# Windowed attention on Trainium2: one sequence over all key groups, v by token as weights, maps scaled before their transposes

## The reference

```python
B_HEADS = D_MODEL // HEAD_DIM          # 16, HEAD_DIM = 64
B_KV_HEADS = 4;  B_GROUP = 4
WINDOW = 128;  Q_BLOCK = 128;  CTX_LEN = 256
...
    def block(args):                    # one block of 128 queries, all groups
        qb, i = args
        ...
        s_band = jnp.einsum('bqhgd,bjhd->bhgqj', qb, kb).astype(f32) * ATTN_SCALE   # 384 neighbours
        s_band = jnp.where(mask, s_band, NEG_INF)
        s_ctx = jnp.einsum('bqhgd,bjhd->bhgqj', qb, kc).astype(f32) * ATTN_SCALE    # 256 context keys
        p = sink_softmax(jnp.concatenate([s_ctx, s_band], axis=-1)).astype(vb.dtype)
        return (jnp.einsum('bhgqj,bjhd->bqhgd', p[..., :n_ctx], vc)
                + jnp.einsum('bhgqj,bjhd->bqhgd', p[..., n_ctx:], vb))
    ...
    out_x = ox.swapaxes(0, 1).reshape(B, S, B_WIDTH) * jax.nn.silu(gx)
```

## Time and profile before

| | us |
|---|---|
| median of 3 runs | 3408.12 (3401.91 to 3419.62) |
| the profiled execution | 3403.24, span 3401.4 |
| PE busy | 3033.2 (89%) |
| DVE busy | 1758.4 (52%) |
| ACT busy | 967.5 (28%) |
| POOL busy | 1038.8 (31%) |

### The profile page before, as it was taken

How to read it: one execution, slowest core, us unless ns; L and a number is a source line. 1 busy time by engine, 2 the same in 40 slices (tenths; PEclk the granted TensorE clock), 3 DMA queues, 4 the chain that set the end, 5 groups by cost and what they waited for, 6 DMA issues and landing times. The chain is left out here.

```text
span 3401.4 us, 45638 instructions
## 1 busy us (share of the span) xinstructions
PE 3033.2 (89%) x16755; PEld 2580.1 (76%) x16755; DVE 1758.4 (52%) x2527; ACT 967.5 (28%) x1574; POOL 1038.8 (31%) x609
## 2 busy tenths in 40 slices
PE   3799978999999999989999988888896999788898
PEld 2678867877777777777878878878785777777786
DVE  5554234375445544455565257878625430555553
ACT  2122234231111111131111137767602001444431
POOL 1533300364454445423222212322333423000022
PEclk9899878999999999999999989999998999888899
DMA  2454232111111111123353322121110332222201
GB/s 81 154 167 137 79 87 68 37 61 45 37 49 54 45 37 49 31 69 114 118 170 138 110 85 86 55 87 48 34 38 6 124 121 74 58 57 57 69 28 66
DMA packets 207430, 257.50 MB, mean 76 GB/s; under 512 B 8969, under 2 KB 173102, under 8 KB 207294
## 3 DMA queue, kind: packets, MB, share of 16 engines
q1 hardware_dynamic: 191430, 190.99, 19.0%
q10 hardware_dynamic: 15872, 64.82, 4.8%
HBM read 188.87 MB, written 66.91 MB: 75 GB/s over the span
## 5 line engine op out<-in xcount | busy, mean ns | idle before, releaser
L858 PE MATMUL ps<-hh,w_parts 128*128 128x512 f32 (+2 forms) x2608 | 1020.1, 391 | 77.7 <-POOL hl L708 32.7
L859 PE MATMUL ps<-hl,w_parts 128*128 128x512 f32 (+2 forms) x2608 | 1003.3, 385 | 0.0
L860 PE MATMUL ps<-hh,w_parts 128*128 128x512 f32 (+2 forms) x2608 | 1000.8, 384 | 0.0
L669 POOL TENSOR_TENSOR w_parts<-w_raw,zero 128x1024 fp32r<-128x1024 f32 x140 | 297.7, 2127 | 1161.5 <-PE ps L860 860.5
L858 PEld LDWEIGHTS ps<-hh,w_parts 128*128 128x128 f32 x2608 | 498.9, 191 | 196.4 <-issue 68.7
L859 PEld LDWEIGHTS ps<-hl,w_parts 128*128 128x128 f32 x2608 | 501.1, 192 | 106.7 <-issue 6.0
L860 PEld LDWEIGHTS ps<-hh,w_parts 128*128 128x128 f32 x2608 | 499.4, 192 | 101.6
L671 POOL TENSOR_TENSOR w_parts<-w_raw,w_parts 128x1024 fp32r<-128x1024 f32 x140 | 339.6, 2425 | 11.0
L2415 DVE TENSOR_SCALAR_CACHE_REDUCE b_s<-ps 128x640 f32<-128x640 f32 (+1 forms) x128 | 101.3, 791 | 245.3 <-PE ps L1353 244.7
L1694 ACT ACTIVATE f_y<-f_z,convv 128x1024 f32<-128x1024 f32 x44 | 54.7, 1244 | 532.8 <-DVE f_z L2242 532.7
L858 PE MATMUL ps<-f_hi,d_hi 128*128 128x512 f32 x352 | 139.5, 396 | 20.1 <-DVE res L2279 14.0
(11 more groups left out here) (317 smaller groups left out, 4949.8 us busy)
## 6 DMA issues: line engine op xcount, KB each, us to landing
w_mod_sb<-in_w_mod SPq DMA_DIRECT2D x16, 1536.0 KB, 7.1
w_raw<-in_w_up SPq DMA_DIRECT2D x44, 512.0 KB, 3.8
w_raw<-in_a_w_in SPq DMA_DIRECT2D x32, 512.0 KB, 4.0
d_raw<-in_w_down SPq DMA_DIRECT2D x22, 512.0 KB, 4.1
w_raw<-in_w_in SPq DMA_DIRECT2D x20, 512.0 KB, 4.8
za_parts<-z_hi ACTq DMA_DIRECT2D x16, 640.0 KB, 3.0
za_parts<-z_lo ACTq DMA_DIRECT2D x16, 640.0 KB, 4.1
d_even<-za_parts SPq DMA_DIRECT2D x16, 640.0 KB, 6.8
```

The lines of the kernel that those rows point to most:

```text
L669: pool.tensor_tensor(wh[:, s], w_raw[:, s], zero[:].broadcast_to([P, KT * P]), ALU.add).then_inc(w_high[s], 1)
L858: pe.matmul(out_, w_hi, x_hi, start=start, stop=False)
L859: pe.matmul(out_, w_hi, x_lo, start=False, stop=False)
L860: return pe.matmul(out_, w_lo, x_hi, start=False, stop=stop)
```

## The change

1. `b_v` is projected by token (`project_by_token`): the activations are the weights of the product and the projection's weights are the moving operand, so v comes out with tokens on the partitions and ACT and DVE write it straight into `b_v`. Both slots of weights are used until the last token. v is neither stored to DRAM nor loaded nor transposed.
2. The loop over the groups becomes one sequence of 128 units. q is loaded in four pieces as the group before frees them, k into two buffers laid over the two slots of `w_parts`, the gate for all groups into `hl`.
3. The scores run 4 units ahead (`BA_LEAD`), `b_s` has 4 buffers in place of 3.
4. The sums are inverted for two units at a time (`ba_norm`), and GpSimd multiplies the map by it in place (`ba_scale`), before the transposes.
5. The mix handles the four heads of a block together, one block behind: v is the weights (64 columns), the transposed maps of two heads the moving operand (256 columns), and the two pairs of heads go to the lower and the upper 64 partitions of the output. The output comes out transposed, so the two transposes of `b_o` go.
6. The first split of `b_out` moves into GpSimd's stream at unit 104.

```diff
+BA_UNITS = 4 * QB * 4
+BA_LEAD = 4
+BA_MIX = ((0,), (1, 2), (3,), (4,))
...
+        b_pt = alloc(scope, "b_pt", [P, 2, 5, 4, P])
...
-        b_v = alloc(scope, "b_v", [P, TOK // 2 // P, 2, DH])
...
-        b_s = alloc(scope, "b_s", [P, 3, 5 * P])
-        b_pt = alloc(scope, "b_pt", [P, 2, 5, P])
...
+        b_v = alloc(scope, "b_v", [P, TOK // P, 4 * DH])
+        b_s = alloc(scope, "b_s", [P, BA_LEAD, 5 * P])
...
+        b_ks = [w_parts[:, p].rearrange("p a n -> p (a n)")[:, 0:2 * TOK].rearrange("p (a n) -> p a n", n=TOK) for p in range(2)]
...
-                sp.wait_ge(ba.scored, 32 * h + 1)
...
+            for s in range(2):
+                sp.wait_ge(stored[s], 16 * Z0["b_gate"][s] + 16)
+            for c in range(4):
+                ba_load_q(0, c)
+            for h in range(2):
+                sp.wait_ge(w_used[h], W0["b_out"][h] + 1)
+                ba_load_k(h)
+            for s in range(2):
+                sp.wait_ge(stored[s], 16 * (Z0["b_gate"][s] + 4) + 16)
+            for h in range(4):
+                ba_load_gate(h)
+            for h in range(1, 4):
+                for c in range(4):
+                    sp.wait_ge(ba.scored, 4 * QB * (h - 1) + 8 * (c + 1))
+                    ba_load_q(h, c)
+                if h < 3:
+                    ba_load_k(h + 1)
...
+            def ba_scale(u):
+                w = len(window_tiles(ba_unit(u)[1])) * P
+                pool.wait_ge(ba.normed, 2 * (u // 2) + 2)
+                pool.tensor_scalar(b_s[:, u % BA_LEAD, 0:w], b_s[:, u % BA_LEAD, 0:w], b_rec[:, 1, u % 4:u % 4 + 1], None, ALU.mult).then_inc(ba_scaled, 1)
...
+                cols = slice(CTX + i * P, CTX + (i + 1) * P)
+                pool.wait_ge(ba_kept, 2 * b + 2)
+                pool.tensor_tensor(hl[:, 2 * h:2 * h + 2, cols], b_y[:, b % 2], hh[:, 2 * h:2 * h + 2, cols].bitcast(F32), ALU.subtract).then_inc(ba.low, 1)
+
+            for u in range(BA_UNITS + 6):
+                if u < BA_UNITS:
+                    ba_scale(u)
+                if u == 4 * QB * 3 + 8:
+                    split(pool, W0["b_out"], 0, 0)
+                if u >= 9 and u % 4 == 1:
+                    ba_keep_low((u - 9) // 4)
+            split(pool, W0["b_out"], 0, 1)
...
+        def project_by_token(pe, name):
+
+            parts = w_parts[:, :, 1:3]
+            for s in range(2):
+                pe.wait_ge(acc_free[s], A0[name][s] + 1)
+                pe.wait_ge(w_split[s], W0[name][s] + 1 + 1)
+            for t in range(TOK // P):
+                if t >= 5:
+                    pe.wait_ge(acc_free[(t - 5) % 2], A0[name][(t - 5) % 2] + (t - 5) // 2 + 1 + 1)
+                tok = slice(t * P, (t + 1) * P)
+                got = bank(t % 5).rearrange("p (s w n) -> p s w n", s=2, w=2)
+                for k in range(KT):
+                    wk = slice(k * P, (k + 1) * P)
+                    if k == KT - 1:
+                        pe.matmul(got[:, :, 0], hl[:, k, tok], parts[:, :, 0, wk], start=False, stop=False)
+                    if k == KT - 1 and t == TOK // P - 1:
+                        for s in range(2):
+                            pe.matmul(got[:, s], hh[:, k, tok], parts[:, s, :, wk], start=False, stop=(s == 1)).then_inc(w_used[s], 1)
+                    else:
+                        last = pe.matmul(got, hh[:, k, tok], parts[:, :, :, wk], start=(k == 0), stop=(k == KT - 1))
+                    if k < KT - 1:
+                        pe.matmul(got[:, :, 0], hl[:, k, tok], parts[:, :, 0, wk], start=False, stop=False)
+                if t < TOK // P - 1:
+                    last.then_inc(v_turned, 1)
 
...
-            project(pe, "b_v", 2, ALL_SEGS)
+            project_by_token(pe, "b_v")
...
-                    for n, kt in enumerate(tiles):
-                        last = pe.matmul(bank(6 + i % 2)[:, a * DH:(a + 1) * DH], b_pt[:, u % 2, n, :], b_v[:, kt % 5, kt // 5, :],
-                                         start=(n == 0), stop=(n == len(tiles) - 1))
...
+            def ba_turn(u):
+                tiles = len(window_tiles(ba_unit(u)[1]))
+                pe.wait_ge(ba_scaled, u + 1)
+                for b, batch in enumerate((range(3), range(3, tiles))):
+                    if u:
+                        pe.wait_ge(ba_copied[b], u)
+                    for n in batch:
...
+                for c in range(2):
+                    last = pe.matmul(bank(6 + b % 2)[c * DH:(c + 1) * DH, 0:2 * P].rearrange("p (t q) -> p t q", t=2),
+                                     b_v[:, tiles[n], h * DH:(h + 1) * DH], b_pt[:, b % 2, n, c::2], start=(n == 0), stop=(n == len(tiles) - 1))
...
-                def ba_turn_output(i):
-                    pe.wait_ge(ba.normed, 24 * h + (3 * i + 3))
...
+            for u in range(BA_LEAD):
+                ba_scores(u)
+            for u in range(BA_UNITS + 4):
+                if u + BA_LEAD < BA_UNITS:
+                    ba_scores(u + BA_LEAD)
+                if u < BA_UNITS:
                     ba_turn(u)
...
+                if u >= 4:
+                    for n in BA_MIX[u % 4]:
+                        ba_mix(u // 4 - 1, n)
...
+                act.activation(b_s[:, u % BA_LEAD, 0:w], b_s[:, u % BA_LEAD, 0:w], ACT.Exp, bias=b_bias[:, r:r + 1], scale=-1.0,
+                               accum_out=b_sum[:, r:r + 1]).then_inc(ba.exped, 1)
+                act.activation(b_sunk[:, r:r + 1], sinks[:, head:head + 1], ACT.Exp, bias=b_bias[:, r:r + 1]).then_inc(ba.exped, 1)
...
+            def ba_norm(p):
+                r = slice(2 * p % 4, 2 * p % 4 + 2)
+                dve.wait_ge(ba.exped, 4 * p + 4)
+                if p >= 2:
+                    dve.wait_ge(ba_scaled, 2 * (p - 2) + 2)
+                dve.tensor_tensor(b_rec[:, 0, r], b_sum[:, r], b_sunk[:, r], ALU.add).then_inc(ba.normed, 1)
+                dve.wait_ge(ba.normed, 2 * p + 1)
+                dve.reciprocal(b_rec[:, 1, r], b_rec[:, 0, r]).then_inc(ba.normed, 1)
...
+                dve.tensor_copy(b_pt[:, b % 2, 3:tiles, a], bank(5)[:, 0:(tiles - 3) * P].rearrange("p (k q) -> p k q", q=P)).then_inc(ba_copied[1], 1)
...
+                dve.tensor_tensor(b_y[:, b % 2], bank(6 + b % 2)[:, 0:2 * P].rearrange("p (t q) -> p t q", t=2),
+                                  hl[:, 2 * h:2 * h + 2, cols].bitcast(F32), ALU.mult).then_inc(ba_kept, 1)
...
+            for u in range(BA_UNITS + 6):
+                if u < BA_UNITS:
+                    if u % 2 == 1 and u + 2 < BA_UNITS:
+                        ba_norm((u + 1) // 2)
+                    if u + BA_LEAD < BA_UNITS:
+                        ba_max(u + BA_LEAD)
                     ba_copy(u)
```

More of the change, by code:

```diff
@@ new lines, in ba_turn @@
+            def ba_turn(u):
[5 more added lines that the diff above has]
+                    for n in batch:
+                        last = turn_tile(bank(4 + b)[:, (n - batch.start) * P:(n - batch.start + 1) * P], b_s[:, u % BA_LEAD, n * P:(n + 1) * P], False)
+                    last.then_inc(ba_turned[b], 1)
@@ new lines, in _ @@
+            for s in range(2):
+                act.wait_ge(stored[s], 16 * Z0["b_gate"][s] + 16)
+            for t in range(TOK // P):
+                if t < TOK // P - 1:
+                    act.wait_ge(v_turned, 24 + t + 1)
+                else:
+                    act.wait_ge(w_used[1], W0["b_v"][1] + 1 + 1)
+                act.activation(b_v[:, t].rearrange("p (s n) -> p s n", s=2),
+                               bank(t % 5).rearrange("p (s w n) -> p s w n", s=2, w=2)[:, :, 1], ACT.Copy).then_inc(v_copied, 1)
@@ new lines, in _ @@
+            for u in range(BA_LEAD):
+                ba_exp(u)
+            for u in range(BA_UNITS):
+                b, a = divmod(u, 4)
+                act.wait_ge(ba_turned[0], u + 1)
+                if b >= 2:
+                    act.wait_ge(ba.mixed, b - 1)
+                act.activation(b_pt[:, b % 2, 0:3, a], bank(4)[:, 0:3 * P].rearrange("p (k q) -> p k q", q=P), ACT.Copy).then_inc(ba_copied[0], 1)
+                if u + BA_LEAD < BA_UNITS:
+                    ba_exp(u + BA_LEAD)
@@ new lines, in _, with ba_max @@
+            for t in range(TOK // P):
+                dve.wait_ge(v_copied, 24 + t + 1)
+                to = b_v[:, t].rearrange("p (s n) -> p s n", s=2)
+                dve.tensor_tensor(to, bank(t % 5).rearrange("p (s w n) -> p s w n", s=2, w=2)[:, :, 0], to, ALU.add).then_inc(acc_free[t % 2], 1)
+            def ba_max(u):
+                h, i, a = ba_unit(u)
+                r, at, w = u % 4, (2 * (u % 2) + 1) * BANK - CTX, len(window_tiles(i)) * P
+                dve.wait_ge(ba.scored, u + 1)
+                if u >= BA_LEAD:
+                    for z in range(2):
+                        dve.wait_ge(ba_turned[z], u - BA_LEAD + 1)
+                dve.tensor_scalar(b_s[:, u % BA_LEAD, 0:w], ps[:, at:at + w], -SCALE, HIGHEST, ALU.mult, ALU.min,
+                                  accum_out=b_low[:, r:r + 1]).then_inc(ba.maxed, 1)
+                dve.wait_ge(ba.maxed, 2 * u + 1)
```

(4 more changed lines are left out.)

280 lines of the change are left out of this document (104 added, 176 removed).

## The result

The change made the kernel slower. In the same comparison the changed kernel takes 3461.33 us (median of 4, 3448.55 to 3480.25) and the kernel before 3411.45 us: ratio 1.0152, 95% interval 1.0097 to 1.0206. I had forecast 3295 us.

What follows compares the result with a forecast made beforehand. TensorE's instruction count bounds the groups, loads the gaps between. From `b_v` to `b_out`, 125.2 + 6.2 + 268.0 + 3 + 4.3 = 406.7 us replaces 516.3; with clock −110.5, 3292.7 from 3403.2, stated as 3295, range 3262 to 3340.

Steps and rivals of the forecast that it cites:

- the wait behind which TensorE's mix and next scores are queued is that for `ba_scaled`: Attention blocks: TensorE's work queues behind the scaling; 0.3 us added to its 8.5 us, giving 8.8 us per middle block.
- 4 S + 0.68 us: GpSimd's work per middle block: four scalings plus the low part, 5.9 us at 1.3 us a scaling.
- S: GpSimd's scaling of one 640-element map: 1.3 us, bounds 0.63 and 1.7, read from two-input operations.
- Rival 2: Attention: the ring or in-order queues bind, TensorE idles, a block takes 10 us; +38 us, 3333 us; chance 9%.
- k ... is some 8 us: hidden: First group's loads: k's 1.3 MB starts one tile (11.2 us) before the gate ends, takes some 8 us, hidden.
- So all four gaps go: Between groups: TensorE's four waits for loads, 69.8 us together, the longest 25.2 us, disappear.
- The start: Start of the attention sequence: 6.2 us from first score to first map transposes, once in place of four starts.
- v by token: Projection of v ahead of the gate: 28.8 us of products plus 2.9 us waiting for a bank.
- The ring S + 2.7: Attention dependency chain per pair of units: scaling, transposes, maximum, copy, inversion, hand-overs; 4.0 us, 8.0 per block.
- the 0.3 us that I had added as waiting: Middle block of attention: allowance for TensorE waiting on the scaling, raising 8.5 us to 8.8.
- rival 1: Mix: column halves do not overlap, TensorE's block 10.4 us; +49 us, 3344 us; chance 17%.
- Rival 3: Attention: GpSimd's scaling binds, slower than before from S = 2.9 us; 3473 us at S = 3.5; chance 3%.

Runs made afterwards that it cites:

- x1: Changed kernel with GpSimd's low part of a block's output two units later in its queue: 3342.8 us, ratio to before 0.980.
- x3: Changed kernel with the low part two units later and SyncE's wait for gate stores ahead of q's first load removed: 3328.18 us, 0.977.
- y2: x3 with GpSimd's scaling written as a product of two tensors, the reciprocal broadcast along the row: 3309.18 us, 0.972.
- w1: y2 with ScalarE's wait for the last gate tile's store moved behind its first four exponentials: 3298.01 us, 0.971.
- x4: Changed kernel with GpSimd scaling only 16 columns of each map, waits and queue order kept: 3359.42 us, 0.986.
- z3: x3 with the scaling moved from GpSimd to VectorE, right behind the inversion: 3316.48 us, 0.975.
- z2: Changed kernel with the two-tensor scaling alone, low part and loads left as they were: 3412.79 us, 1.0048.

## Why the prediction was wrong

The direction was wrong, at 96% confidence, by a kernel whose arithmetic was mostly right. From the changed kernel at 3461 us the runs lead back to the forecast in four steps: the low part's place 118.5 us (x1), q's wait 14.6 (x3 against x1), the kind of scaling instruction 19.0 (y2 against x3), the first exponential's wait 11.2 (w1 against y2). That arrives at 3298, and I had said 3295. So close a hit is partly luck: in w1 the stretch from `b_v` to `b_out` is 414.5 us, against 406.7 forecast, and the kernel before stood at 3401 us in that comparison, 10 below the 3411 of the result.

**The step that failed** is the one on what is queued behind waiting instructions. It named only TensorE's work, "the wait behind which TensorE's mix and next scores are queued is that for `ba_scaled`". GpSimd got a load (5.9 us per block, below TensorE's 8.5), and its queue was looked at for the split at unit 104 alone. But the change puts the scaling, on which every transpose depends, into the same in-order queue as the low part, and the low part waits for VectorE. Before, that wait was 389.9 us in all and harmless, because nothing urgent stood behind it. The row was in my own list; I read it as slack, and it was the warning. In GpSimd's block of "4 S + 0.68 us" the stop is the missing term: 3.9 us in the mean, and with S at 1.89 and the waits for inversions the block is 13.4 us in place of 5.9. Neither the stop nor the scaling's length makes the loss by itself: without the stop (x1), and with the scaling nearly gone (x4), the kernel is over 100 us faster. Rival 2 spoke of "in-order queues", but looked for them at VectorE's copy and priced a block at 10 us; the middle blocks measure mostly 13.4 to 13.6.

**The loads.** "k ... is some 8 us: hidden" and "So all four gaps go" failed for the first load. Three gaps went. The first stayed, at 21.7 us, because SyncE had a wait that the diff leaves as it was, ahead of q. I priced the transfer and not what its issue waits for, though the rule to look at each queue that a step is moved past would have led there. It is worth 14.6 us by the medians of x1 and x3.

**The size of S.** 1.3 us was forecast, 1.7 the upper bound, 1.89 measured. I took it from the two-tensor rows, and a multiplication by a per-row scalar is another instruction. With the two-tensor form the row was right (1.25). As a term it is 19 us where the queue doesn't stop, 48.5 where it does. The Trainium skill ("GPSIMD Engine Reference", the per-element model) gives 1.03 cycles per element, an estimate of 0.55 us for 640; the trace disagrees with that by a factor above three.

**The start.** 6.2 us to the first transposes were forecast. In y2 it is 13.9, with 7.9 for a store that ScalarE waits for and 1.3 for the table, neither of which I had listed; in w1 it is 6.7.

**What was right.** v by token 33.0 (31.7), the wait for a whole split ahead of the gate 4.41 (4.3) and no wait for it at `b_out` (1.6 us remain, for the last low part). The column halves overlap, 0.44 us per tile (0.43), and a piece costs some 0.24 us for both switches (0.2). The ring S + 2.7 holds in x3. And a stage bound by TensorE is what y2 shows: a middle block takes 8.78 us (8.8), and TensorE is busy for all of it, so that the 0.3 us that I had added as waiting is work. The attention takes 292.4 us against 281.5, of which 7.7 are the late start. One argument for rival 1 was wrong in itself: the scores are not "bound by instruction", since the forecast's own edge block takes 0.055 us off each product for 128 columns less.

**Rival 3** (GpSimd binds, slower than before) had the right sign for another reason. Its condition was S above 2.9 us, and S is 1.89. x1 excludes the load as the whole cause: GpSimd is as busy there (255 us) and the kernel 118 us faster.

**Open.** v by token, some 8.6 us more on the path than the old `b_v` by these rows, was not tried by itself. That the 19 us ahead of `b_v` are scatter rests on the clock in one execution.

## What to carry to other kernels

When a change gives an engine with an in-order queue its first urgent instruction, list what else stands in that queue and what each of those instructions waits for: an idle engine with a long wait in the profile is the sign to look, not room to spare. Then add the stop to that engine's work per round: a stop that a lightly loaded engine makes good costs the whole kernel once the sum is longer than the round. An instruction that nobody needs soon belongs behind the point at which its input is surely there; here two places in the queue were worth 118 us. And where a load is moved, read what its queue waits for ahead of it, in the lines that the diff does not show as well.

## What the runs showed of the hardware

On GpSimd a float32 multiplication by a per-row scalar took 1.89 us for 640 columns, 1.57 for 512 and 0.33 for 16, 2.5 ns per column; by a broadcast tensor it took 1.25 for 640 and 1.04 for 512.

VectorE's cast of 256 columns, 0.30 us in the changed kernel, where GpSimd stands still beside it, became longer when GpSimd's scaling ran at the same time. In x3 the group reads (count, busy us, mean ns):

```profile
L2519 DVE CAST hh<-s_y 128x256 fp32r<-128x256 f32 x32 | 20.9, 655 | 1.1
```

In y2 its mean is 491 ns, and the product out of PSUM ahead of it stays at 0.41 in all of them. In z3, where GpSimd doesn't scale, the cast is back at 295 ns. The Trainium skill ("SBUF — State Buffer", Terms) has the two engines share a pair of ports, which one holds for its full instruction while the loser is blocked. The trace agrees that the two disturb each other in this form, but not that the loser waits for the whole instruction. In x3 a cast begins and ends inside a pair of scalings:

```profile
3009.42 3.75 POOL L875 TENSOR_SCALAR b_s<-b_s,b_rec 128x640 f32<-128x640 f32 x2 [0.88 <-DVE b_rec L2498]
...
3011.50 0.72 DVE L2519 CAST hh<-s_y 128x256 fp32r<-128x256 f32 x1
```

The second scaling begins at 3011.3 and ends at 3013.2; the cast has ended at 3012.2.

The granted clock over the attention went with TensorE's waits for the scaling: 0.85 in the changed kernel (39 waits, 92.8 us, the longest 3.0), 0.91 in z2 (39, 72.3 us, 2.3), 0.99 in x4 (32, 42.8 us, 1.4), and 0.98 in x1 without the stop. In the changed kernel the lower clock made up two fifths of the stop's price (48.9 of 118.7 us).
